# Input projection of a hybrid decoder layer: the root mean square taken out of the operand and applied behind the projections, bias tables read skewed from DRAM

## The reference, cut to what matters

```
h = x * rsqrt(mean(x*x) + eps) * norm1_g          # per token
p = h @ w_in                                      # columns for three head groups
A: 6 DeltaNet heads:  q,k,v = silu(causal_conv4(p_qkv)); o = norm(delta_rule(q,k,v,beta,g)) * silu(p_z)
B: 4 dilated heads:   softmax(q k^T * hd**-0.5 + table[bucket(i-j)]) v
C: 6 sparse heads, 2 shared k/v groups: compressed, selected and windowed branches, with the same kind of table
beta, g and the sparse heads' gates come from 30 further columns of p
x = x + concat(A,B,C) @ w_out;  then norm, gated MLP with a convolution, residual, final norm
```

## Time and profile before

| what | value |
|---|---|
| median of 3 runs | 2793.23 us (2792.86 to 2794.67) |
| the profiled execution | 2789.81 us, of which its span 2788.0 us |
| mean granted TensorE clock over the span | 0.975 of full |
| PE busy | 2628.1 us (94%) |
| DVE busy | 1315.3 us (47%) |
| ACT busy | 874.3 us (31%) |
| block 1 (first to last matmul of it) | 7.28 to 62.48 us |
| head 0's first work that needs its convolutions (L539) | 115.32 us |
| first matmul of the dilated heads (L860) | 598.96 us |

### The profile page before, as it was taken

One profiled execution on the slowest core, in us unless ns is written; L12 is line 12 of the kernel. 1 busy time (PEld: TensorE's weight loads), 2 busy tenths in 40 slices (PEclk: granted clock), 3 DMA queues, 4 the chain that ended last, 5 costly groups with the idle time before them and its releaser, 6 DMA issues.

```text
span 2788.0 us, 33817 instructions
## 1 busy us (share of the span) xinstructions
PE 2628.1 (94%) x12024; PEld 2124.7 (76%) x12024; DVE 1315.3 (47%) x2196; ACT 874.3 (31%) x1628; POOL 77.0 (3%) x54
## 2 busy tenths in 40 slices
PE   6999989889999886998999999999999999999997
PEld 4777777777788553886888888888888888888886
DVE  5555666633244555334444444444344444444444
ACT  3433333323234333223332223232223232323223
POOL 0001111100000000000000000000000000000002
PEclk9999999999999996998999999999999999999999
DMA  6111111112235001521322222222222223222222
GB/s 239 72 65 34 60 64 64 49 65 98 76 117 208 14 38 68 204 99 57 110 101 98 97 91 91 106 94 103 91 91 91 102 95 106 91 92 103 91 94 91
DMA packets 44219, 259.34 MB, mean 93 GB/s; under 512 B 5136, under 2 KB 7056, under 8 KB 15292
## 3 DMA queue, kind: packets, MB, share of 16 engines
q1 hardware_dynamic: 44092, 257.62, 25.7%
HBM read 245.37 MB, written 12.23 MB: 92 GB/s over the span
## 4 chain that ended last, share of the span: by engine, by line
PE 52%; DVE 0%; ACT 0%; issue 0%; DVEq 0%; ACTq 0%
PE bank L221 34%; PE bank L1502 18%; ACT fin_squares L1606 0%; DVE xs L1649 0%; DVE xs L1648 0%; DVE xs L1564 0%; DVEq L1467 0%; ACT fin_rs L1609 0%; ACT L1609 0%; DVE fin_rs L1643 0%; ACTq L1605 0%; DVEq L1628 0%
## 5 line engine op out<-in xcount | busy, mean ns | idle before, releaser
L221 PE MATMUL bank<-h_hi,w_hi 128*128 128x512 f32 x2272 | 915.4, 403 | 12.2 <-DVE w_lo L182 6.9
L221 PE MATMUL bank<-h_lo,w_hi 128*128 128x512 f32 x2272 | 889.3, 391 | 0.0
L221 PE MATMUL bank<-h_hi,w_lo 128*128 128x512 f32 x2272 | 888.5, 391 | 0.0
L182 DVE TENSOR_TENSOR w_lo<-w_raw,w_hi 128x512 fp32r<-128x512 f32 x840 | 557.4, 711 | 470.5 <-ACT w_hi L173 468.9
L173 ACT ACTIVATE w_hi<-w_raw 128x512 fp32r<-128x512 f32 x840 | 489.5, 624 | 707.5 <-PE bank L1502 314.9
L221 PEld LDWEIGHTS bank<-h_hi,w_hi 128*128 128x128 f32 x2272 | 429.4, 189 | 103.0 <-issue 10.2
L221 PEld LDWEIGHTS bank<-h_lo,w_hi 128*128 128x128 f32 x2272 | 428.7, 189 | 91.8
L221 PEld LDWEIGHTS bank<-h_hi,w_lo 128*128 128x128 f32 x2272 | 429.5, 189 | 86.7 <-issue 3.2
L1502 PE MATMUL bank<-w_lo,g_hi 128*128 128x512 f32 x704 | 279.1, 396 | 0.0
L1502 PE MATMUL bank<-w_hi,g_lo 128*128 128x512 f32 x704 | 279.1, 396 | 0.0
L1502 PE MATMUL bank<-w_hi,g_hi 128*128 128x512 f32 x704 | 279.1, 396 | 0.0
(11 more groups left out here) (274 smaller groups left out, 1992.3 us busy)
## 6 DMA issues: line engine op xcount, KB each, us to landing
w_raw<-in_weights SPq DMA_DIRECT2D x210, 1024.0 KB, 4.8
xs<-in_x SPq DMA_DIRECT2D x4, 1024.0 KB, 13.6
mix_scratch<-head_out SPq DMA_DIRECT2D x16, 256.0 KB
xs<-in_x SPq DMA_DIRECT2D x1, 4096.0 KB, 17.7
out<-xs SPq DMA_DIRECT2D x4, 1024.0 KB, 6.1
nsa_tab<-toeplitz_scratch SPq DMA_DIRECT2D x1, 2688.0 KB, 11.2
xs<-bias_scratch SPq DMA_DIRECT2D x10, 256.0 KB, 5.1
toeplitz_scratch<-xs SPq DMA_DIRECT2D x10, 256.0 KB
```

Source lines behind the costliest of these rows:

```text
L182: nc.vector.tensor_tensor(w_lo[:, s, :], raw_quarter(dve_q), w_hi[:, s, :].bitcast(F32), ALU.subtract).then_inc(lo_done, 1)
L221: m = nc.tensor.matmul(PB[pb][:], a[:, s, k], b[:, kt, :], start=(kt == 0 and n == 0), stop=(kt == KT - 1 and n == 2))
```

## The change

x comes in transposed from the host (`x_t`: channels on partitions, tokens along the row), so that block 1 has no transposes. Each k-tile is multiplied by its channel's `norm1_g`, a per-partition scalar, and split at once; the token's 1/rms is left out. Squares are summed over the k-tiles on ACT and DVE, a matmul with ones sums over the partitions, and root and reciprocal give `r_row` (1/rms along the row, the same on all partitions); four transposes give `r_col` (tokens on partitions). These factors are applied where projections are read from PSUM. The ten rows of biases are now made in block 2, stored 128 times each to DRAM in one transfer (a source with stride 0), and the tables are read from there with a row pitch of one element less than the row, once for the dilated and once for the sparse heads, one DMA for each head. The reversal matmuls, their copies and stores are gone.

```diff
+        def load_table(sp, tab, heads, width):
+            for i, h in enumerate(heads):
+                src = bass.AP(tensor=rows_d, offset=h * P * YLEN + P - 1, ap=[[YLEN - 1, P], [1, width]])
+                sp.dma_start(tab[:, i, :], src).then_inc(table_in, 16)
+        X_PIECES = ((0, 2), (2, 4), (4, 8), (8, 12), (12, 16))
...
 # block 1, SP
+                sp.dma_start(g1[:], t["g1"]).then_inc(g1_in, 16)
+                x_piece(0)
+                load_unit(sp)
+                for i in range(1, len(X_PIECES)):
+                    x_piece(i)
+                load_unit(sp)
                 sp.dma_start(cst[:], t["cst"]).then_inc(const_in, 16)
...
 # block 1, ACT
+                for i, (a, e) in enumerate(X_PIECES):
+                    act.wait_ge(x_in[i], 16)
+                    for kt in range(a, e):
+                        nc.scalar.activation(h_hi[:, kt, :], xt[:, kt, :], ACT.Copy, scale=g1[:, kt:kt + 1])\
+                            .then_inc(xh_hi, 1)
+                    if i < 2:
+                        split_hi(act, 2)
+                split_hi(act, 1)
+                for c in range(4):
+                    nc.scalar.activation(sq[:, 4 * c:4 * c + 4, :], xt[:, 4 * c:4 * c + 4, :], ACT.Square).then_inc(sq_a, 1)
+                    if c < 3:
+                        split_hi(act, 1)
...
 # block 1, DVE: the same order, h_lo by scalar_tensor_tensor(xt, g1, h_hi), then
+                for c in range(1, 4):
+                    split_lo(dve, 1)
+                    dve.wait_ge(sq_a, c + 1)
...
+                    nc.vector.tensor_tensor(sq[:, 0:4, :], sq[:, 0:4, :], sq[:, 4 * c:4 * c + 4, :], ALU.add)\
+                        .then_inc(ss_v, 1)
...
 # block 1, PE
+                for u in range(2):
+                    for kt in range(KT):
+                        if u == 0:
+                            pe.wait_ge(xh_lo, kt + 1)
+                        project(pe, u, kt)
...
+                for k in range(4):
+                    m = nc.tensor.matmul(W[3][:], ones, sq[:, k, :], start=(k == 0), stop=(k == 3))
+                m.then_inc(ss_ps, 1)
...
 # block 2, SP, behind the four small loads
+                sp.dma_start(bl[:], t["bias_lhs"]).then_inc(bias_in, 16)
+                sp.dma_start(oh[:], t["onehot"]).then_inc(bias_in, 16)
+                load_units(sp, 4)
+                sp.wait_ge(rev_sb, 2)
+                sp.dma_start(rows_d.ap()[:, :, :], rev[:, None, :].to_broadcast([DIL_H + NSA_H, P, YLEN]))\
+                    .then_inc(stored, 16)
                 for h in range(DN_H):
                     load_units(sp, (16 + 16 * min(h + 1, DN_H - 1) + 12 * (h == DN_H - 1) + AHEAD + 3) // 4)
...
 # block 2, PE
-                fill = filler(pe, 4, first=1)
-                fill(12)
+                fill = filler(pe, 4, first=2)
+                fill(4)
                 small_pe(pe)
+                bias_pe(pe)
                 fill(4)
+                rms_turn_pe(pe)
                 small_turn_pe(pe)
-                fill(14)
+                fill(10)
                 cumulate_pe(pe)
                 fill(1000)
...
 # block 2, ACT
+                rms_act(act)
+                split_hi(act, 4)
                 act.wait_ge(in_small, 32)
                 nc.scalar.activation(sw_hi[:], sw[:], ACT.Copy).then_inc(sm_hi, 1)
                 small_act(act)
-                split_hi(act, 6)
+                split_hi(act, 2)
...
 # block 2, DVE (rms_dve: reciprocal of r_row; bias_dve: two copies of 10x512, then rev_sb is 2)
+                rms_dve(dve)
+                split_lo(dve, 4)
                 dve.wait_ge(sm_hi, 1)
                 nc.vector.tensor_tensor(sw_lo[:], sw[:], sw_hi[:].bitcast(F32), ALU.subtract).then_inc(sm_lo, 1)
+                bias_dve(dve)
                 small_dve(dve)
                 dve.wait_ge(par_in, 32)
-                split_lo(dve, 6)
+                split_lo(dve, 2)
...
 # conv_steps, for each of q, k, v
-                    step(nc.vector.tensor_scalar(B[n][:], PB[i][:], cw[:, i, 3:4], None, ALU.mult))
+                    if i or not (isinstance(h, int) and h == 0):
+                        dve.wait_ge(conv_v, 3 * h + i)
+                    nc.vector.tensor_tensor(B["cr"][:], PB[i][:], r_row[:], ALU.mult).then_inc(raw_v, 1)
+                    yield
+                    dve.wait_ge(raw_v, 3 * h + i + 1)
+                    step(nc.vector.tensor_scalar(B[n][:], B["cr"][:], cw[:, i, 3:4], None, ALU.mult))
                     yield
...
 # dn_act: silu(z) now behind the copy of AT, in place; dn_dve, behind T's two instructions:
+                dve.wait_ge(q_used, 16 * h + 16)
+                nc.vector.tensor_tensor(B["zs"][:], PB[3][:], r_row[:], ALU.mult).then_inc(z_free, 1)
...
 # dn_dve, between chunks
-                    for _ in range(3):
+                    for _ in range(4):
                         next(convs, None)
...
 # dilated heads, ACT
-                nc.scalar.activation(ks[:], PB[1][:], ACT.Copy).then_inc(kv_ev, 1)
...
-                nc.scalar.activation(vt[:].rearrange("p b n -> p (b n)"), W[3][:], ACT.Copy).then_inc(vt_ev, 1)
 # dilated heads, DVE
+                nc.vector.scalar_tensor_tensor(qs[:], PB[0][:], SCALE, r_row[:], ALU.mult, ALU.mult).then_inc(q_ev, 1)
+                nc.vector.tensor_tensor(ks[:], PB[1][:], r_row[:], ALU.mult).then_inc(k_ev, 1)
                 split_lo(dve, 2)
-                dve.wait_ge(table_in, 16 * len(PIECES) + 16)
+                dve.wait_ge(vtr_ps, n + 1)
+                nc.vector.tensor_tensor(vt[:], W[3][:].rearrange("p (b n) -> p b n", b=TB), bc(r_col[:], P), ALU.mult)\
+                    .then_inc(vt_ev, 1)
+                dve.wait_ge(table_in, 16 * DIL_H)
...
 # sparse heads: the eight k tiles leave PSUM on DVE with r_row, the four v tiles on ACT as before and,
 # turned, on DVE with r_col; q with r_row; the tables by load_table in six DMAs
```

More of the change, by code:

```diff
@@ L59 @@
 LEVELS = (2, 4, 8, 16, 32, 64)
-(K_ID, K_ONE, K_TRI, K_ML, K_MU, K_M1, K_M1T, K_REV) = range(8)
-K_LV = 8
+(K_ID, K_ONE, K_TRI, K_ML, K_MU, K_M1, K_M1T) = range(7)
+K_LV = 7
 N_CST = K_LV + len(LEVELS)
@@ L312, in normalize @@
             return act_part, dve_part, pe_part, y_v, lo
-        toep_d = nc.dram_tensor("toeplitz_scratch", (DIL_H + NSA_H, P, TW_NSA), F32).ap()
-        PIECES = [(h, 0, QW) for h in range(DIL_H + NSA_H)] + [(h, QW, TW_NSA - QW) for h in range(DIL_H, DIL_H + NSA_H)]
-        ROUNDS = (PIECES[:8], PIECES[8:])
-        with ExitStack() as c1, nc.Block() as block:
[L323 to L337, removed]
+        STORED2 = 16
@@ L360, in _, with x_piece @@
[L360 to L363, removed]
+                def x_piece(i):
+                    a, e = X_PIECES[i]
+                    sp.dma_start(xt[:, a:e, :], t["x_t"][:, a:e, :]).then_inc(x_in[i], 16)
+                sp.dma_start(g1[:], t["g1"]).then_inc(g1_in, 16)
+                x_piece(0)
@@ L372, in _ @@
                 act.wait_ge(const_ready, 2)
-                n1_act(act)
-                split_hi(act, AHEAD + 4)
             @block.vector
             def _(dve):
[L378 to L385, removed]
+                dve.wait_ge(g1_in, 16)
@@ new lines, in _ @@
+                for i, (a, e) in enumerate(X_PIECES):
+                    for kt in range(a, e):
+                        dve.wait_ge(xh_hi, kt + 1)
+                        nc.vector.scalar_tensor_tensor(h_lo[:, kt, :], xt[:, kt, :], g1[:, kt:kt + 1],
+                                                       h_hi[:, kt, :].bitcast(F32), ALU.mult, ALU.subtract)\
+                            .then_inc(xh_lo, 1)
+                    if i < 2:
+                        split_lo(dve, 2)
+                split_lo(dve, 1)
@@ L387, in _ @@
+                for c in range(1, 4):
+                    split_lo(dve, 1)
+                    dve.wait_ge(sq_a, c + 1)
+                    if c > 1:
+                        dve.wait_ge(ss_v, c - 1)
+                    nc.vector.tensor_tensor(sq[:, 0:4, :], sq[:, 0:4, :], sq[:, 4 * c:4 * c + 4, :], ALU.add)\
+                        .then_inc(ss_v, 1)
             @block.tensor
             def _(pe):
[L389 to L398, removed]
-                pe.wait_ge(const_in, 16)
[L400 to L407, removed]
@@ L470, in cumulate_pe, with rms_act, rms_dve, rms_turn_pe @@
                 nc.tensor.matmul(W[3][:, 0:DN_H * TB], cst[:, K_ONE, :], flat, start=True, stop=True).then_inc(g_cum, 1)
+            def rms_act(act):
+                act.wait_ge(ss_ps, 1)
+                nc.scalar.activation(r_row[:], W[3][:], ACT.Sqrt, bias=eps_t[:], scale=1.0 / D_MODEL).then_inc(r_root, 1)
+            def rms_dve(dve):
+                dve.wait_ge(r_root, 1)
+                nc.vector.reciprocal(r_row[:], r_row[:]).then_inc(r_ok, 1)
+                dve.wait_ge(r_ok, 1)
+            def rms_turn_pe(pe):
+                pe.wait_ge(r_ok, 1)
+                for b in range(TB):
```

(21 more changed lines are left out.)

109 lines of the change are left out of this document (58 added, 51 removed).

## The result

The changed kernel takes **2864.32 us** (median of 4 runs, 2858.71 to 2864.86), the kernel before 2793.05 us beside it (4 runs, 2792.00 to 2794.67): a ratio of 1.025, interval 1.0232 to 1.0268. The forecast was 2854, with 2787 to 2868 as range. The span is 2862.2 us against 2788.0, the mean granted clock 0.961 against 0.975.

A forecast was written before the change was run, and what follows sets the result against it. TensorE, busy 94% of the span, was taken as the bound. Terms 52.2 + 6.6 + 1.5 + 0.5 = 61 us on 2789.8 gave 2851; with the median 3.4 above, 2854 us, range 2787 to 2868.

The forecast's parts named there:

- The store: Bias rows' store from ten partitions: four neighbours share a path, so 79 us, with unit 4 queued behind it; chance 0.57.
- Rival 1: Bias rows' store: each partition has an engine to itself, 20 us, whole kernel 2795 us; chance 0.20.
- Rival 3: Bias rows' store: runs at the 35 GB/s of the 34-partition load, 150 us, whole kernel 2925 us; chance 0.05.
- rival 4: Bias rows' store: slow, but only 30 to 60 us, whole kernel 2804 to 2835 us; chance 0.11.
- The opening: Everything ahead of head 0's convolution-dependent work: this mark moves from 115.3 to 167.5 us, +52 us.
- TensorE's stand: During the bias rows' store: TensorE runs out of filling work and is idle from about 86 us on.
- DeltaNet heads: DeltaNet stage: more VectorE steps between chunks and the multiply for z, together +6.6 us, between 0 and 9.
- Both terms: DeltaNet heads: four VectorE steps instead of three between chunks, 3.6 us in five heads; multiply for z, 0.5 six times, 3.
- Dilated heads: Dilated stage: k follows q on VectorE, 0.6 us each, v's turn near a fill's end; +1.5 us, between -1 and 4.
- Sparse heads and the rest: Sparse stage: k tiles (8 x 0.69 us) lie under units of 11 us; +0.5 us for all of it.

The follow-up runs named there:

- experiments 1 to 3: Changed kernel with another source for the rows' store: 1, partitions 12 apart, 2804.18 us; 2, 4 apart, 2825.36; 3, same bytes from 128 partitions, 2790.16.
- experiments 5 and 6: Kernel with the store in eight parts, but: 5, DeltaNet convolutions without r_row, 2782.60 us; 6, SiLU of z on ScalarE without r_row, 2784.06 (one profiled execution each).
- experiment 7: Kernel with the store in eight parts, but dilated k and v copied by ScalarE without their factors: 2781.72 us in one profiled execution.
- Experiment 8: Changed kernel with rows 12 apart, store in eight parts, units 2 and 3 loaded in block 1, one unit ahead of the dilated tables: 2772.91 us.
- experiment 4: Changed kernel with the rows' store in eight parts, each issued behind one unit of weights, still from partitions 0 to 9: 2787.18 us.

## Why the prediction was right, step by step

**The store.** Right in mechanism and size. From its issue to unit 4's landing 84 us were predicted, 79 of them the store; 86.4 were measured to that unit's first split, and the four rows on a path account for 79.1. The two flat stretches have the rates of three paths and of two, and experiments 1 to 3 move the time as the rows on the fullest path say. Rival 1 (an engine for each partition) needed 250 GB/s or more: that came only when the rows were put apart. Rival 3's 150 us and rival 4's 30 to 60 are not what was measured.

**The opening.** Block 1 ends at 37.3 (predicted 36.5), TensorE starts again at 49.57 (48), the reciprocal of 3.35 us lies in this stand (39.62), the store is issued at 69.53 (67), and unit 4 is split at 155.91, where 151 for its landing plus a start was meant. From there to the mark are 17.5 us (16.2; the 167.5 of the prediction is 0.3 more than its terms 151 and 16.2 add up to). VectorE in order of time, the first of the three convolutions:

```profile
161.26 0.68 DVE L676 TENSOR_TENSOR dn_cr<-bank,rms_row 128x512 f32<-128x512 f32 x1
161.98 0.48 DVE L679 TENSOR_SCALAR dn_qp<-dn_cr,dn_cw 128x512 f32<-128x512 f32 x1
162.50 2.32 DVE L683 SCALAR_TENSOR_TENSOR dn_qp<-dn_cr,dn_cw,dn_qp 128x511 f32<-128x511 f32 x3
```

3.66 us from one to the next where I had 3.45; the durations of the forms held to 0.01 us, the waits between them are longer. All small steps erred to the same side, +58.1 in place of +52.

**TensorE's stand** began at 89.0 (86 predicted).

**DeltaNet heads.** +8.1 in place of +6.6, inside the 0 to 9 given. TensorE's waits in this stage grew by 5.5 us, from 48.2 to 53.7; the other 2.6 are within what the stage scatters. The wait for `vn` grew by 2.8 us (some 3 predicted). Both terms had the right size, some 3 us each by the waits of experiments 5 and 6 (3.6 and 3 predicted). But z's has it by luck: the wait that it was priced at, for T's first update, did not grow (8.8 us before, 8.4 in the changed kernel); its cost came at the masked scores (2.3) and at splits (3.6), and about half of this was given back elsewhere.

**Dilated heads.** The term that was mis-sized: +1.5 predicted, bounded by 4, measured +5.7. Within the stage TensorE's waits grew by 4.6 us. I priced q and k one behind the other, and that was right (1.8 more, 1.7 by experiment 7). What I put at nothing is the wait at the first head's logits, none before and 2.8 us in the changed kernel: I had v's turn near the end of a fill and the tables landing under fills. But the first unit is issued behind their four DMAs, and VectorE splits that unit, and scales v's turn, ahead of the logits. The last 1.1 us are longer busy time of TensorE (258.1 and 259.2 us). SyncE issues the unit at 665.31, as the stage begins (665.21), where the kernel before had it on its way at 597.33, 1.6 us before its stage. ScalarE's first split and VectorE's last step on the first logits, before and then in the changed kernel:

```profile
604.92 1.15 ACT L173 ACTIVATE w_hi<-w_raw 128x512 fp32r<-128x512 f32 x2 [5.52 <-DMA w_raw<-in_weights]
610.67 0.29 DVE L899 TENSOR_SCALAR dil_lg<-dil_lg,dil_den 128x128 f32<-128x128 f32 x1
```

```profile
673.06 1.15 ACT L173 ACTIVATE w_hi<-w_raw 128x512 fp32r<-128x512 f32 x2 [7.57 <-DMA w_raw<-in_weights]
679.41 0.29 DVE L952 TENSOR_SCALAR dil_lg<-dil_lg,dil_den 128x128 f32<-128x128 f32 x1
```

Counted from the stage's first matmul (598.96 and 665.21), that step comes after 11.7 and 14.2 us. Of the 2.5 us between them 1.9 are there already at the first split (after 6.0 and 7.9 us), which starts 7.6 and 7.8 us after the unit's issue in both: this is the unit's place. The other 0.6 are v's turn on VectorE. Experiment 8 moves the unit alone: with k and v still on VectorE the split starts 3.4 us after the first matmul and the step comes after 12.0, though VectorE now waits 2.1 us for the tables.

**Sparse heads and the rest.** +0.5 predicted; +2.9, then -0.6 behind it. TensorE's waits in the sparse stage are the same, 51.0 us before and 51.1 after, and the +2.9 lie in its busy time (201.6 and 204.3 us), at 0.89 and 0.88 of full clock; this is within what the stage scatters with the same code (last section).

Sum: 58.1 + 8.1 + 5.7 + 2.9 - 0.6 = 74.2 of the two profiled executions, against 61. Of the medians the difference is 71.3, since the profiled run before was 3.2 us below its median and the one after 0.2.

## What to carry to other kernels

Before a store from a few partitions, count how many of its rows fall on the same group of four neighbours (and the four 32 further on): in these runs that number, not the total, set its time, and a matmul with a spread-out left side puts the rows apart at no cost that these runs show. A long transfer that nobody needs soon belongs behind, or in parts between, the loads that the next work waits for, when all go through one queue. A factor moved out of an operand comes back at every place that reads the result; count these places on the engine that is already on the path between two matmuls.

## What the runs showed of the hardware that was not expected

**The clock of a later stage differs between kernels with the same code there.** The sparse stage is the same in the changed kernel and in experiment 4, with the same waits (37.3 and 37.9 us for the logits, 5.5 and 5.4 for the compressed scores). Its main part, from the first compressed scores to the output projection, columns as in the earlier trace rows, first the changed kernel, then experiment 4:

```profile
987.10:1189.30 202.20, 155.82 (x588) 98.57 (x588) 108.20 (x297) 79.66 (x229) 0.00 (x0) 0.85 0.10 36
```

```profile
910.20:1106.00 195.80, 149.05 (x589) 95.29 (x589) 108.06 (x297) 79.59 (x229) 0.00 (x0) 0.88 0.10 37
```

6.4 us apart at 0.85 and 0.88 of full clock, with 6.8 us less of PE's busy time for the same instructions. The stage as a whole (from the compression on) is 250.8 and 251.3 us long at 0.91 in experiments 3 and 4, and 255.1 to 257.9 at 0.88 or 0.89 in the other seven kernels that have this code, while TensorE's waits in it add up to 49.7 to 51.8 us in all nine. So what differs is how much of TensorE's work fell on the slow level; what decides that is not shown. A difference under some 7 us in the total can be this alone, and is read by stages; the profiled executions of experiments 3 and 4 owe some 4 to 7 us to it.

**The stand costs more than itself.** TensorE was granted 0.50 through the whole of 110 to 173.4 us: the four matmuls at the mark took 1.06 us where they took 0.66 before.
